# The feed-forward of the second block's first layer as 2 by 2 blocks with Strassen's seven products, and six conditioning groups between gates

## What is computed

```python
def _conv_ffn(h, p):
    u = _depthwise_conv(h @ p['ffn_wup'], p['ffn_dw'], p['ffn_db'])
    g, v = jnp.split(u, 2, axis=-1)
    return (jax.nn.silu(g) * v) @ p['ffn_wdown']

def _trunk_layer(x, xc, mod, cmod, p, cos, sin, last):
    shift1, scale1, gate1, shift2, scale2, gate2 = [m[:, None, :] for m in jnp.split(mod, 6, axis=-1)]
    ...
    x = _layer_norm(DN_ALPHA * x + gate2 * _conv_ffn(x * (1 + scale2) + shift2, p), p['ln2_g'], p['ln2_b'])
    if last:
        return x, None
    ...
    xc = _layer_norm(DN_ALPHA * xc + cgate2 * _conv_ffn(xc * (1 + cscale2) + cshift2, p), p['ln2_g'], p['ln2_b'])
    return x, xc
```

## Time and profile before

| | |
|---|---|
| Time, median of 3 runs | 2923.6 us (2921.12 to 2939.53) |
| Profiled execution | 2926.9 us, of which its span is 2925.1 us |
| Busy: TensorE, VectorE, ScalarE, GpSimd | 96%, 42%, 23%, 3% of the span |
| Mean granted clock of TensorE | 0.982 |
| Weights moved | 300.58 MB on SyncE's queue |
| Feed-forward of layer 0, up and down | about 1590.5 to 2060.2 us of the span |

### The profile page before, as it was taken

The page is one execution under the profiler, slowest core; times in us unless marked ns, Lnnn a source line. Parts: engine busy times, 40 slices in busy tenths (PEclk is TensorE's granted clock), DMA queues, the critical chain, the costliest instruction groups (busy, mean ns, idle before and its releaser), DMA issues. The chain is left out here.

```text
span 2925.1 us, 31664 instructions
## 1 busy us (share of the span) xinstructions
PE 2821.2 (96%) x12884; PEld 1822.3 (62%) x12884; DVE 1229.9 (42%) x2494; ACT 661.6 (23%) x1236; POOL 85.8 (3%) x115
## 2 busy tenths in 40 slices
PE   9988999999999999999999999999998999999997
PEld 8747788844774444654444444444457877788886
DVE  7852233013881017758524222211227328754332
ACT  2132122022541020330112212200225222222220
POOL 0000000001230000000000000000002100000000
PEclk9989999999999999999999999999999999999999
DMA  5362544423003222102222342222220332244442
GB/s 206 131 223 74 209 152 150 151 98 116 29 30 115 73 71 79 37 29 79 101 72 94 130 158 101 79 72 79 105 72 32 106 127 89 79 144 134 154 151 94
DMA packets 85679, 309.24 MB, mean 106 GB/s; under 512 B 9328, under 2 KB 11376, under 8 KB 85280
## 3 DMA queue, kind: packets, MB, share of 16 engines
q1 hardware_dynamic: 84032, 300.58, 30.0%
q0 software_dynamic: 1504, 6.64, 0.6%
HBM read 306.14 MB, written 1.05 MB: 105 GB/s over the span
## 5 line engine op out<-in xcount | busy, mean ns | idle before, releaser
L500 PE MATMUL ps<-sb 128*128 128x256 f32 (+1 forms) x7088 | 2131.8, 462 | 6.3 <-DVE sb L566 3.7
L500 PEld LDWEIGHTS ps<-sb 128*128 128x128 f32 x7088 | 1345.9, 190 | 778.6 <-issue 646.4
L2213 DVE SCALAR_TENSOR_TENSOR sb<-sb 128x512 f32<-128x512 f32 (+1 forms) x480 | 275.5, 616 | 8.7
L2505 DVE SCALAR_TENSOR_TENSOR sb<-sb 128x512 f32<-128x512 f32 (+1 forms) x176 | 101.0, 616 | 334.8 <-ACT sb L2478 333.3
L2477 ACT COPY sb<-ps 128x512 f32<-128x512 f32 (+1 forms) x88 | 42.2, 479 | 352.6 <-PE ps L500 340.5
L2439 DVE SCALAR_TENSOR_TENSOR sb<-ps,sb 128x256 f32<-128x256 f32 x48 | 21.7, 481 | 229.4 <-PE ps L500 229.4
L1403 PE MATMUL ps<-sb 128*128 128x512 f32 x256 | 110.4, 593 | 0.0
L2328 ACT ACTIVATE sb<-sb 128x512 f32<-128x512 f32 (+1 forms) x32 | 15.6, 523 | 371.9 <-DVE sb L2366 371.9
L1403 PEld LDWEIGHTS ps<-sb 128*128 128x128 f32 x256 | 48.5, 190 | 61.8 <-issue 61.8
L1309 DVE SCALAR_TENSOR_TENSOR sb<-sb 128x256 f32<-128x256 f32 x88 | 38.8, 482 | 105.4 <-ACT sb L1285 104.7
L1702 POOL TENSOR_TENSOR sb<-sb 128x256 f32<-128x256 f32 x84 | 70.6, 877 | 387.3 <-ACT sb L1630 387.3
(11 more groups left out here) (373 smaller groups left out, 2205.5 us busy)
## 6 DMA issues: line engine op xcount, KB each, us to landing
sb<-in_w SPq DMA_DIRECT2D x567, 512.0 KB, 3.3
sb<-in_two POOLq DMA_DIRECT2D x2, 1088.0 KB, 8.0
sb<-in_x SPq DMA_DIRECT2D x2, 512.0 KB, 4.1
sb<-in_ctx POOLq DMA_DIRECT2D x1, 1024.0 KB, 8.6
sb<-in_v_bias POOLq DMA_DIRECT2D x2, 512.0 KB, 3.8
out_xt<-sb SPq DMA_DIRECT2D x1, 1024.0 KB, 4.8
sb<-in_par SPq DMA_DIRECT2D x1, 764.0 KB, 6.7
sb<-in_s5b POOLq DMA_DIRECT2D x1, 512.0 KB, 7.6
```

Source lines behind the costliest of these rows:

```text
L500: ins = pe.matmul(o[:, i * n:(i + 1) * n], w, rhs(k), start=(k == 0), stop=(k == kt - 1))
L2213: ve.scalar_tensor_tensor(out=o_, in0=s_, scalar=pc(("conv_dw", l, j), m + e), in1=o_, op0=ALU.mult, op1=ALU.add).then_inc(vector_steps, V ...
L2505: ve.scalar_tensor_tensor(out=o_, in0=z2[e][:, g, 0:c, j:j + TX], scalar=pc(("ffn_dw", l, j), g * FT + m), in1=o_, op0=ALU.mult, op1=ALU.a ...
```

## The change

Strassen's scheme in Winograd's form multiplies two 2 by 2 block matrices with seven block products instead of eight, at the price of sums of blocks. In layer 0 alone (`BLOCKED = ('l0',)`):

- **Up** (tiles 1 to 21, `t_up_blocks`): the weight block rows are the gate's and the value's 128 output channels, its columns the two halves of the 1024 input channels (four weight tiles each); the activation's blocks are those two halves by two halves of the 512 columns (x and context). Each product is four matmuls of 256 columns. Four sums of the weights are made by VectorE in each tile (`v_block_sums`), one of them in place in the ring; four sums of H once, before tile 1 (`v_up_turns`). Six of the seven products go one after another through two banks, `b` (P1, P6, P7, P4) and `c` (P5, P3), where they accumulate; bank `a` holds P2. ScalarE copies `b` out between its products (`a_up_part`), VectorE joins the parts into `z2` (`v_up_parts`). The middle tap is now made from `z2`, not from the bank (`a_center2`).
- **Down** (`t_down_blocks`): four pairs of output tiles, each over three k blocks (`DOWN`: halves of 4, 4 and 3 tiles). The seven products of a pair lie in five banks. VectorE makes the sums of u2 as its tiles come (`v_down_turns`), the weight sums per block, and joins the products with the residual (`v_down_parts`).
- In the layer norm behind it `sqsum`'s last step comes after the last tile's centring.
- The six conditioning groups of the up projection go to the loop over `t_glu` in `t_mla_in` (after its tiles 3 and 5, `ADA_GLU`) and before tiles 2 and 5 of the branches 0 and 1 (`ADA_BRANCH`); what brings layer 1's result out stands around tiles 2 to 4.

```diff
+        def v_block_sums(key, buf, free):
...
+            half = lambda s, q: ring[:, s % RING, 4 * q:4 * q + 4, :]
+            ve.tensor_tensor(buf[:, 0], half(s2, 0), half(s2, 1), ALU.add).then_inc(vector_steps, V.step(("S1", key)))
+            ve.wait_ge(vector_steps, V.n)
+            ve.tensor_tensor(buf[:, 1], buf[:, 0], half(s1, 0), ALU.subtract).then_inc(vector_steps, V.step(("S2", key)))
+            ve.tensor_tensor(half(s2, 0), half(s1, 0), half(s2, 0), ALU.subtract).then_inc(vector_steps, V.step(("S3", key)))
+            ve.wait_ge(vector_steps, at(("S2", key)))
+            ve.tensor_tensor(buf[:, 2], half(s1, 1), buf[:, 1], ALU.subtract).then_inc(vector_steps, V.step(("S4", key)))
...
+        def t_up_blocks(f, m):
...
+            part_product(b, a11, src(0, 0), True).then_inc(tensor_jobs, T.step(("job", (key, "P1"))))
...
+            pe.wait_ge(vector_steps, at(("S1", key)))
...
+            part_product(c, sums[0], turn(0), True).then_inc(tensor_jobs, T.step(("job", (key, "P5"))))
+            pe.wait_ge(vector_steps, at(("S2", key)))
+            pe.wait_ge(scalar_steps, at(("P1", key)))
+            part_product(b, sums[1], turn(1), False).then_inc(tensor_jobs, T.step(("job", (key, "P6"))))
+            a = open_job((key, "a"))[:, 0:hn]
+            part_product(a, a12, src(1, 0), True).then_inc(tensor_jobs, T.step(("job", (key, "a"))))
+            pe.wait_ge(vector_steps, at(("S3", key)))
+            pe.wait_ge(scalar_steps, at(("P6", key)))
+            part_product(b, a21, turn(2), False).then_inc(tensor_jobs, T.step(("job", (key, "P7"))))
+            pe.wait_ge(vector_steps, at(("S4", key)))
+            pe.wait_ge(scalar_steps, at(("P5", key)))
+            part_product(c, sums[2], src(1, 1), False).then_inc(tensor_jobs, T.step(("job", (key, "c"))))
+            pe.wait_ge(scalar_steps, at(("P7", key)))
+            part_product(b, a22, turn(3), False).then_inc(tensor_jobs, close_job((key, "b")))
...
             for m in range(FT):
-                if m == 0:
+                if blocked and m:
+                    t_up_blocks(ffn2[l], m)
+                elif m == 0:
...
-                if l == 0 and m % 2 and ada_done[0] < 2 * ADA:
-                    more_ada()
...
+                for m in range(1, FT):
+                    a_up_part(f, m, 0)
+                    if m >= 2:
+                        a_center2(l, n, m - 1)
+                    for i in range(1, 4):
+                        a_up_part(f, m, i)
                     a_silu2(l, n, m - 1)
+                    a_up_close(f, m)
...
+                for m in range(1, FT):
+                    if m + 1 < FT:
+                        up_sums(f, m + 1)
+                    else:
+                        down_sums(f, 0)
+                    v_conv2(l, n, m - 1)
+                    v_up_parts(f, m)
+                    v_mul2(l, n, m - 1)
+                    v_down_turns(f, m - 1)
```

More of the change, by code:

```diff
@@ L204, in build @@
 def build(nc, t_in, out, known):
-    table, stream, slab_last, job_of = {}, [], {}, {}
+    table, stream, slab_last, job_of, slab_at = {}, [], {}, {}, {}
     ctx = ExitStack()
@@ L489, in tile4, with block_row @@
             return ring[:, s % RING, i % SLAB:i % SLAB + 4, :].rearrange("p a b -> p (a b)")
+        def block_row(key, name, l, k0, half, c):
+            while len(stream) % SLAB:
+                if len(stream) % SLAB == SLAB - 1:
+                    open_slabs.append(len(stream) // SLAB)
+                stream.append(None)
+            s = len(stream) // SLAB
+            slab_at[key] = s
+            for q in range(2):
+                for i in range(4):
+                    if i < half:
+                        tile(name, l, (k0 + q * half + i) * P, c)
+                    else:
+                        if len(stream) % SLAB == SLAB - 1:
+                            open_slabs.append(s)
+                        stream.append(None)
+            return [[ring[:, s % RING, 4 * q + i, :] for i in range(half)] for q in range(2)]
@@ new lines, in a_center2 @@
+        def a_center2(l, n, m):
+            e, c = m % 2, n // TX
+            if m >= 2:
+                act.wait_ge(vector_steps, at(("u2", l, m - 2)))
+            act.wait_ge(vector_steps, at(("C12", ffn2[l].key(m))))
+            act.wait_ge(scalar_steps, at(("free", (ffn2[l].key(m), "b"))))
+            for g in range(2):
+                act.activation(zb2[e][:, g, 0:n].rearrange("p (a b) -> p a b", b=TX), z2[e][:, g, 0:c, 1:TX + 1], ACT.Identity,
+                               bias=pc(("ffn_db", l), g * FT + m), scale=pc(("ffn_dw", l, 1), g * FT + m)).then_inc(scalar_steps, A.step(("z2", l, m)))
```

306 lines of the change are left out of this document (265 added, 41 removed).

## The result

The changed kernel takes 2890.6 us (median of four runs, 2877.06 to 2894.36), beside 2929.3 us for the kernel before on the same chip (2921.12 to 2939.53, four runs): a ratio of 0.986, interval 0.981 to 0.991. It is faster by 1.4%, and the time lies within the range of 2862 to 2896 us, 17.6 us above the point forecast of 2873. Of the 50.8 us forecast, the medians show 38.7 and the two profiled spans 32.5 (2925.1 to 2892.6).

A forecast was written before the change was run, and what follows sets the result against it. TensorE alone was taken to bound layer 0's feed-forward. -52.8 us there and +2.0 in the tail make -50.8, from a median of 2923.6 to about 2873 us; range 2862 to 2896.

The forecast's parts named there:

- The gain on TensorE, 52.8 us: Layer 0's feed-forward: 1024 records of 512 columns become 1792 of 256, saving 34.6 us up and 18.2 down.
- VectorE's tile: Up projection: VectorE needs 9.5 us of a tile's 12.1 on TensorE, 2.6 to spare, so TensorE never waits.
- hardly elsewhere: Up projection: VectorE would idle before line 650, waiting for bank `c`, about 1 us a tile, and hardly anywhere else.
- rival 2: Handovers between products leave gaps as a copy or sum lands late, 6 to 36 us: 2880 to 2909; chance 0.12.
- rival 3: Weights can't be loaded ahead of a wait, 44 us over 231 products: 2917, no change; chance 0.06.
- rival 4: VectorE becomes the up projection's bound, above 14.5 us a tile; at 16 us 2956, slower; chance 0.03.
- rival 5: VectorE holds the up projection near its old pace, 13 to 14 us a tile: 2892 to 2913; chance 0.03.
- The start and the hand-over to down: VectorE's sums before tile 1 and for down's second k block come in time, hidden by 1.7 and 1.6 us.
- The conditioning groups: 0: Six groups moved out of the up projection cost about 1.9 us each wherever they stand, so no net change.
- The tail, +2.0: After the last down products, later centring and squares delay the layer norm: loss 2.0 us, bounds 1 and 4.
- at +2.7: In the tail, VectorE's centring is done 2.7 us after the last product, instead of 1.8 before the change.
- rival 1: The forecast itself: TensorE stays the bound, the gain comes whole but for the tail: 2864 to 2880; chance 0.76.

The follow-up runs named there:

- groups_only: Only the six conditioning groups moved, no product blocked, against the kernel before: 2935.2 us, ratio 1.001.
- both_layers: Seven products in layer 1's feed-forward too (moving blocks of 128 columns), against the changed kernel: 2868.9 us, ratio 0.979 to the kernel before.

## Why the prediction was right, and where not

**The gain on TensorE, 52.8 us: right.** 52.95 by the marks against groups_only (52.64 from tile 1 on), 34.75 up (34.6) and 17.94 down (18.2). The step that carried it was reading 0.2158 us for a record of 256 columns from a long run of the kernel before. The grouped lines of the changed kernel, tile 1 to the mean, shapes apart, confirm the count (1791 from 1636 us on, and the first record started at 1635.41) and that nothing was waited for (the last column, idle time before, and what ended it):

```profile
L552 PE MATMUL ps<-sb 128*128 128x256 f32 x1791 | 387.1, 380 | 0.0
...
L567 DVE TENSOR_TENSOR sb<-sb 128x512 f32<-128x512 f32 x32 | 22.1, 692 | 1.1
L565 DVE TENSOR_TENSOR sb<-sb 128x512 f32<-128x512 f32 x32 | 22.0, 689 | 52.2 <-PE ps L552 48.4 <-DMA sb<-in_w 3.7
...
L648 DVE TENSOR_TENSOR sb<-sb 128x256 f32<-128x256 f32 x21 | 8.9, 425 | 32.2 <-ACT sb L628 32.2
...
L650 DVE TENSOR_TENSOR sb<-sb,ps 128x256 f32<-128x256 f32 x21 | 8.8, 421 | 18.7 <-PE ps L552 18.7
```

**VectorE's tile: right in size, its idle time partly elsewhere.** The sums take 0.69 us and the joins 0.42, as read from the earlier trace rows. Before L650 VectorE idles 18.7 / 21 = 0.9 us, where I said about 1; before L648 it idles another 1.5 for ScalarE's copy, which I had not placed; so "hardly elsewhere" was wrong. ScalarE's two `Identity` activations took 1.52 us together, and not twice 0.63. None of this delays TensorE. Rivals 2, 3, 4 and 5 did not come about: no idle time at L552, and no gap between products.

**The start and the hand-over to down: right.** The four differences of 1024 elements took 1.22 us each (between 0.69 and 2.29, 1.25 taken); the first sum was there at 1634.5, before tile 1's start at 1635.4. The second k block's second sum was done at 1902.97, 13.0 us after the last up product (1635.41 + 1176 x 0.2158 + 0.81 for L1615 = 1890.0; 13.9 said), and needed at +15.5.

**The conditioning groups: 0, right.** They gave 12.3 us in the stretch and cost 12.3 at the new places. The part of the span that holds them now grew by 13.4 in the first profile; from kernel to kernel that figure goes from 8 to 13.5, though the groups are the same. In the first profile 1.7 of it is the clock behind a wait that both kernels have; the other differences stay open.

**The tail, +2.0: right in kind, too certain in size.** The step that failed is centring "at +2.7": it ended at +3.3, since three joins, two residuals and the centring take 3.2 us one after another (2024.05 to 2027.28), and the squares ended at +4.1 in place of +3.4. It cost 2.5 us where the clock held and 4.7 where it fell, the second above the bound of 4; counted to the end of the next layer's first tile it is 3.1 and 4.3. That the engine's idle time there can halve the clock stood in the earlier trace rows as 0.81; I had it as a small supplement and not as a second outcome.

**The level of the kernel before: the step that failed, and two pieces of luck.** The sum was set against a median of three runs, 2923.6, as if this were one level with some scatter. The three were 2921, 2924 and 2940: two of the lower set and one of the upper. My profile of before had the full clock in the serial stretch, so 2873 was a forecast for executions of that kind. They came out at 2873.3 (median of three), but that near a hit is luck: the lower set of before lies at 2920.9, 2.7 below the 2923.6 that I started from, and the gain is 3.2 less than the 50.8. The other nine of twelve come out at 2892.3, and the first four runs, with three of that kind, at 2890.6. This is outside rival 1's window (2864 to 2880), to which I had given 0.76, and inside that of rival 2 (2880 to 2909), of which nothing came about. The mechanism was rival 1's; that the measured median lies in the range is owed to room that was there for another reason. The range's lower end was also miscalculated: 2921.1 less 52.8 is 2868.3, not 2862. Set against set the gain is 47.6 and 43.6 us and not 50.8. The tail (up to 2.7 us more than the 2.0) and the clock ahead of tile 0 can hold what is missing, but only profiled executions show either, so how much each holds in the medians is open. The hint was in the three times: two within 2.5 us, and the third 16 above them.

## What to carry to other kernels

Where TensorE alone is the bound and VectorE has the time for the sums (here it was busy for 170 of 253 us), seven products in place of eight give their eighth almost whole, down to moving blocks of 256 columns; at 128 columns nearly half of it is lost to the shorter records and to waits. Price the records from a long run of the same width, and each handover from the idle time of the engine that makes the sums. Before comparing two kernels by 1 or 2%, look for stretches of small matmuls with idle times of about 1 us: their clock may differ from run to run. A few useless matmuls there steadied both kernels, for some 3 us in each.

## What the runs showed of the chip

- A clock that falls by chance: with the same records and the same idle times just before (1.04 and 0.74 us), eight records of 64x128 took 1.05 us in one execution and 1.91 in another, and the clock stayed low for some 40 us. It cost 15 us, by the sets in 31 of 52 executions of the one kernel and 9 of 12 of the other. I had not expected such short idle times to matter, as the earlier trace rows show nothing of the kind in dense work.
- Idle times of 2.2 and 3.0 us in the tail: the matmul pair behind them took 2.08 us (2.22 of idle time), 2.07 and 1.13 (3.01 in both). The same idle time gave both. So did the 2.39 us ahead of the layer norm's mean in the third branch: 1.12 us for the pair before, 1.94 after.
- An FP32 record costs 0.4292 us at 512 columns, 0.2158 at 256 and 0.1120 at 128: over half each time, by 1.2 ns at the first cut and 4.1 ns at the second. The Trainium skill (TensorE: Matmul & The Clock Gate, "Wait — 56ns, not 53.3ns?") has one fixed cost of about 2.5 ns a matmul, by which, as an estimate, each cut would add 1.25 ns to a record. The trace agrees for the first cut; at the second the measured cost is higher, and the measurement decides.
- Weight loads of 191 ns (340.9 us for 1789 in the stretch) stay hidden behind records 216 ns apart, over waits that are met too. Even at 112 ns a record, loads of 192 ns each didn't stop the stream in both_layers.
